# Norm weights folded into the merge, a lower lowest level, and the first score products of a chunk issued before the last one's means

## The reference, cut to what matters

```python
# gated linear attention (GLA: 4 heads of 64 keys; HGRN2: 4 heads of 128), chunk by chunk
b = cumsum(log_decay)
o_inter = (q * exp(b)) @ state
scores[i, j] = sum_d q[i, d] * k[j, d] * exp(b[i, d] - b[j, d])      # for j <= i
o = o_inter + scores @ v
state = state * exp(b_last) + (k * exp(b_last - b)).T @ v
y_gla = rms_norm(o, gla_norm_w) * silu(gr)                          # y_hgrn likewise
# Mamba-2: y = chunked scan of x, gated by silu(z)
y_ssm = rms_norm(y, ssm_norm_w)                                     # in 4 groups of 256 channels
merged = g0 * (y_gla @ w_br_gla) + g1 * (y_hgrn @ w_br_hgrn) + g2 * (y_ssm @ w_br_ssm)
```

## Time and profile before

| | us |
|---|---|
| median of 3 runs | 2038.89 |
| lowest, highest run | 2036.88, 2039.36 |
| span of the profiled execution | 2040.4 |
| what the page gives outside the span | nothing |
| TensorE busy | 1925.7 (94%) |
| VectorE busy | 1472.5 (72%) |
| ScalarE busy | 1048.0 (51%) |

### The profile page before, as it was taken

How to read it: one execution, slowest core, us unless ns; L and a number is a source line. 1 busy time by engine, 2 the same in 40 slices (tenths; PEclk the granted TensorE clock), 3 DMA queues, 4 the chain that set the end, 5 groups by cost and what they waited for, 6 DMA issues and landing times. The chain is left out here.

```text
span 2040.4 us, 26797 instructions
## 1 busy us (share of the span) xinstructions
PE 1925.7 (94%) x10602; PEld 1576.7 (77%) x10603; DVE 1472.5 (72%) x1687; ACT 1048.0 (51%) x1234; POOL 218.3 (11%) x173
## 2 busy tenths in 40 slices
PE   6999999999999999999998999995999999999993
PEld 5789888888977777777776888874788888888881
DVE  5876467667227888788775656556889988999875
ACT  5234344444224545444444334223777887888763
POOL 3310000000030000000001000012122222222210
PEclk9999999999999999999998999997999999999996
DMA  5242332432355557656537654543999999999986
GB/s 168 86 145 73 114 104 97 131 104 93 107 145 158 151 160 168 167 127 152 160 115 282 206 204 182 229 178 138 349 376 384 389 386 385 389 386 387 387 331 259
DMA packets 212415, 436.11 MB, mean 214 GB/s; under 512 B 28018, under 2 KB 151042, under 8 KB 184770
## 3 DMA queue, kind: packets, MB, share of 16 engines
q1 hardware_dynamic: 179394, 355.68, 50.3%
q10 hardware_dynamic: 20864, 53.49, 7.5%
q0 software_dynamic: 12032, 25.22, 3.2%
HBM read 369.67 MB, written 81.43 MB: 221 GB/s over the span
## 5 line engine op out<-in xcount | busy, mean ns | idle before, releaser
L1602 PE MATMUL psum<-h_hi,l_hi 128*128 128x512 f32 x384 | 158.5, 413 | 4.9 <-PEq L58 3.3
L1602 PE MATMUL psum<-h_lo,l_hi 128*128 128x512 f32 x384 | 159.8, 416 | 0.0
L1602 PE MATMUL psum<-h_hi,l_lo 128*128 128x512 f32 x384 | 157.9, 411 | 0.0
L2741 DVE TENSOR_TENSOR gu_lo<-up_raw,gu_hi 128x2048 fp32r<-128x2048 f32 x64 | 146.3, 2288 | 13.2 <-ACT gu_hi L2684 13.2
L2684 ACT CAST gu_hi<-up_raw 128x2048 fp32r<-128x2048 f32 x64 | 122.1, 1909 | 35.0 <-PE u_ps L2813 35.0
L1258 ACT COPY l_out<-psum 128x512 f32<-128x512 f32 x48 | 28.1, 585 | 170.3 <-PE psum L1602 162.3
L2457 PE MATMUL mpsum<-y_hi,wb_hi 128*128 128x512 f32 x256 | 103.3, 403 | 10.1 <-DVE y_lo L2217 9.1
L2813 PE MATMUL g_ps<-gu_hi,xeT_hi 128*128 128x512 f32 x256 | 105.0, 410 | 5.8 <-DVE xeT_lo L2750 5.8
L806 DVE TENSOR_TENSOR w_lo<-w_raw,w_hi 128x512 fp32r<-128x512 f32 x90 | 61.9, 689 | 65.5 <-ACT w_hi L662 65.5
L662 ACT CAST w_hi<-w_raw 128x512 fp32r<-128x512 f32 x90 | 55.7, 622 | 91.9 <-PE ps L931 91.4
L2457 PE MATMUL mpsum<-y_lo,wb_hi 128*128 128x512 f32 x256 | 101.7, 397 | 0.0
(11 more groups left out here) (465 smaller groups left out, 5419.0 us busy)
## 6 DMA issues: line engine op xcount, KB each, us to landing
up_raw<-moe SPq DMA_DIRECT2D x62, 1024.0 KB, 8.1
gate_raw_a<-moe SPq DMA_DIRECT2D x33, 1024.0 KB, 8.4
gate_raw<-moe SPq DMA_DIRECT2D x33, 1024.0 KB, 8.4
dn_raw_a<-moe SPq DMA_DIRECT2D x31, 1024.0 KB, 7.2
dn_raw<-moe SPq DMA_DIRECT2D x31, 1024.0 KB, 8.0
w_raw<-w_in SPq DMA_DIRECT2D x26, 1024.0 KB, 6.1
l_raw<-w_gates ACTq DMA_DIRECT2D x24, 512.0 KB, 5.4
s_gates<-l_out ACTq DMA_DIRECT2D x48, 256.0 KB, 4.0
```

What stands on the lines that cost most here:

```text
L1602: ins = nc.tensor.matmul(psum[:, bank, :], w[t % 2][:, k, :], x[:, k, half * 512:half * 512 + 512], start=i == 0, stop=i == LATE_MM - 1, s ...
L2741: nc.vector.tensor_tensor(gu_lo[p][:], gu_raw[p][:], gu_hi[p][:].bitcast(F32), ALU.subtract).then_inc(gu_ready, 1)
```

## The change

- **Norm weights.** `nw` and `nw_s` become one tile `y_w` that outlives the mixers. `gla_hgrn_out` and `ssm_out` no longer multiply with them: each is one operation over the chunk in place of 8. The merge multiplies instead: `upper_y` and `rest_y` apply them for each 128-channel row block, so each piece takes two operations of 512 columns in place of one of 1024, on ScalarE and on VectorE.
- **Lowest level.** At level h = 1 decay is taken relative to the later token. The query factor is then 1: `dec` makes half as many elements, ScalarE takes one exponential of half and copies the odd keys, VectorE has the key product only, and TensorE reads every second query straight from `q_in`.
- **Diagonal.** Since the copy at level 1 brings the odd keys undecayed, odd queries get their own token's score there; the mask of that level is widened. `diagonal` makes even queries alone: 12 products of the levels' form in place of 16 (in chunk 0, 6 in place of 8), into bank 1 alone, and `diagonal_in` is one copy in place of two. A further mask is made for it on GpSimd.
- **Order.** `relative(c+1, 0)`, `factors(c+1, 0)` and `(c+1, 1)`, two more `dec`, `diagonal(c+1)` and `level(c+1, 0)` move from the next body to the end of this one: on TensorE right behind `intra(c, 0)`, ahead of the filler and the means. On ScalarE `relative(c, 2)` moves ahead of `gla_hgrn_scale(c-1)`, and `relative(c+1, 0)` ahead of the copy of B. On VectorE `scores_in(0)` and `factors(2)` move ahead of `gla_hgrn_out`, and `scores_in(6)` ahead of the decayed queries. A level waits for one score copy less than before.

```diff
     NE = NL + 1
-    NS = NL + 2
+    NS = NL + 1
...
             def relative(c, lv):
                 i, h = NE * c + lv, LEVELS[lv]
+                if h == 1:
+                    act.wait_ge(qk_loaded[c % 2], 80 * turns(c))
+                    if c:
+                        act.wait_ge(sc_ready, NS * c)
+                    pairs = lambda ap: ap.rearrange("p (n w) -> p n w", w=2)
+                    nc.scalar.copy(pairs(k_one[:])[:, :, 1:2], pairs(flat(k_in[c % 2][:]))[:, :, 1:2])
+                    act.wait_ge(d_ready, i + 1)
+                    nc.scalar.activation(ex[i % 3][:, 0:CT * HALF], ex[i % 3][:, 0:CT * HALF], ACT.Exp).then_inc(e_ready, 1)
+                    return
...
             def body(c):
                 b, h0 = c % 2, PREFIX + PER_CHUNK * c
+                relative(c, 2)
                 if c:
                     gla_hgrn_scale(c - 1)
-                relative(c, 2)
...
                 nc.scalar.activation(wmat, wmat, ACT.Exp, scale=-1.0).then_inc(wexp_ready, 1)
+                if c < LAST:
+                    relative(c + 1, 0)
...
                 nc.scalar.activation(flat(ya), o_ps, ACT.Square).then_inc(sq_ready, 1)
                 if c < LAST:
-                    relative(c + 1, 0)
                     relative(c + 1, 1)
...
+                if lv == NL - 1:
+                    view = at[:].rearrange("p a (n w) -> p (a n) w", w=2)
+                    tt(out[:, 0:CT * HALF].unsqueeze(2), view[:, :, 1:2], view[:, :, 0:1], ALU.subtract).then_inc(d_ready, 1)
...
-                for h in range(NH):
-                    ins = stt(ya[:, h, :], g_in[:, h, :], nw[:, h:h + 1], ya[:, h, :], ALU.mult, ALU.mult)
-                ins.then_inc(ya_ready, 1)
+                tt(ya, g_in[:], ya, ALU.mult).then_inc(ya_ready, 1)
...
-                for k in range(8):
-                    ins = stt(yb[:, k, :], yt[:, k, :], nw_s[:, k:k + 1], rs2[:, k // 2, :], ALU.mult, ALU.mult)
-                ins.then_inc(yb_ready, 1)
+                by_group = lambda ap: ap.rearrange("p (g a) t -> p g a t", a=2)
+                tt(by_group(yb), by_group(yt[:]), rs2[:].unsqueeze(2).to_broadcast([P, SSM_GROUPS, 2, CH]), ALU.mult).then_inc(yb_ready, 1)
...
                 i0 = NE * c
-                factors(0)
-                factors(1)
                 if c:
                     dve.wait_ge(o_ready, c)
-                diagonal_in(0)
-                dec(i0 + 3)
-                diagonal_in(1)
-                dec(i0 + 4)
+                diagonal_in()
+                scores_in(0)
+                factors(c, 2)
                 if c:
                     gla_hgrn_out(c - 1)
-                else:
-                    late(3)
-                scores_in(0)
-                factors(2)
-                if c:
                     intra_in(c - 1, 1)
...
                 dec(i0 + 9)
                 dec(i0 + 10)
+                if c < LAST:
+                    factors(c + 1, 0)
+                    dec(i0 + 11)
                 late(h0 + 2)
...
                 intra_in(c, 0)
+                if c < LAST:
+                    factors(c + 1, 1)
+                    dec(i0 + 12)
...
             def body(c):
                 b = c % 2
-                diagonal(c)
                 if c:
                     intra(c - 1, 1)
-                fill(SLOT)
-                level(c, 0)
-                fill(SLOT)
+                fill(2 * SLOT)
                 level(c, 1)
...
                 intra(c, 0)
+                if c < LAST:
+                    diagonal(c + 1)
+                    level(c + 1, 0)
                 fill(SLOT)
...
-                nc.scalar.copy(y_hi[:, q * PK:(q + 1) * PK, :], y_part(p)).then_inc(y_hi_ready, 1)
+                for k in range(q * PK, (q + 1) * PK):
+                    ins = nc.scalar.activation(y_hi[:, k, :], y_part(p)[:, k - q * PK, :], ACT.Copy, scale=y_w[:, k:k + 1])
+                ins.then_inc(y_hi_ready, 1)
...
-                tt(y_lo[:, ks, :], y_part(p), y_hi[:, ks, :].bitcast(F32), ALU.subtract).then_inc(y_ready, 1)
+                for k in range(q * PK, (q + 1) * PK):
+                    ins = stt(y_lo[:, k, :], y_part(p)[:, k - q * PK, :], y_w[:, k:k + 1], y_hi[:, k, :].bitcast(F32),
+                              ALU.mult, ALU.subtract)
+                ins.then_inc(y_ready, 1)
```

More of the change, by code:

```diff
@@ L955, in late_bank, with mixers @@
     return 7
[L958 removed]
+def mixers(nc, io, dr, h_hi, h_lo, l_raw, l_hi, l_lo, w_place, xz_place, y_w, stored, early):
     LEVELS = [64 >> n for n in range(7)]
@@ L1215, in _ @@
             n = 0
-            for lv, h in enumerate(LEVELS):
+            for lv, (h, past) in enumerate([(h, h - 1) for h in LEVELS[:-1]] + [(1, 1), (1, 0)]):
                 nb = CH // (2 * h)
@@ L1227, in _ @@
                 pool.wait_ge(mask_sem, n)
-                nc.gpsimd.affine_select(out=view, in_=view, compare_op=ALU.is_ge, fill=0.0, base=h - 1,
+                nc.gpsimd.affine_select(out=view, in_=view, compare_op=ALU.is_ge, fill=0.0, base=past,
                                         pattern=[[2 * h, nb], [0, h]], channel_multiplier=-1).then_inc(mask_sem, 1)
@@ L1386, in _ @@
                 own.link(nc.vector.memset(k_lv[b][:], 0.0))
-            for lv in range(NL):
+            for lv, to in enumerate(mask + [mask_d]):
                 dve.wait_ge(mask_sem, 3 * lv + 3)
-                nc.vector.tensor_copy(mask[lv][:].rearrange("p (a h) -> p a h", h=HALF),
+                nc.vector.tensor_copy(to[:].rearrange("p (a h) -> p a h", h=HALF),
                                       mask_f[:].unsqueeze(1).to_broadcast([P, NH, HALF])).then_inc(mask_ready, 1)
-            dve.wait_ge(mask_ready, NL)
-            dve.wait_ge(ident_ready, 1)
-            own.link(nc.vector.tensor_copy(mask_d[:].rearrange("p (a h) -> p a h", h=CH),
-                                           ident[:].unsqueeze(1).to_broadcast([P, 4, CH])))
+            dve.wait_ge(mask_ready, NL + 1)
             dve.wait_ge(const_ready, 3)
@@ L1470, in factors, with body, diagonal_in @@
                     tt(ql[:, 2:8], q8[:, 2:8, :, h:2 * h], e6[:, :, :, h:2 * h], ALU.mult).then_inc(qk_ready, 1)
-                def diagonal_in(a):
-                    n = NS * c + a
+            def body(c):
+                b, h0 = c % 2, PREFIX + PER_CHUNK * c
+                def diagonal_in():
+                    n = NS * c
                     dve.wait_ge(sc_ready, n + 1)
@@ L1508, in body @@
                 dec(i0 + 5)
-                factors(3)
+                factors(c, 3)
                 if c:
@@ L1519, in body @@
                 dec(i0 + 6)
-                factors(4)
+                factors(c, 4)
                 late(h0)
@@ L1528, in body @@
                 dec(i0 + 7)
-                factors(5)
+                factors(c, 5)
                 late(h0 + 1)
                 scores_in(4)
-                factors(6)
+                factors(c, 6)
                 dve.wait_ge(xT_ready, c + 1)
@@ L1540, in body @@
                 tt(k_in[b][:], k_in[b][:], ex[(NE * c + NL) % 3][:].rearrange("p (a t) -> p a t", t=CH), ALU.mult).then_inc(qk_ready, 1)
+                scores_in(6)
                 dve.wait_ge(eb6_ready, c + 1)
@@ L1569, in _ @@
             late(1)
+            for lv in range(2):
+                factors(0, lv)
+                dec(lv + 3)
+            late(3)
             for c in range(NCH):
@@ L1607, in _, with one_of_two @@
             SLOT = LATE_MM // 3
+            def one_of_two(q, which):
+                return q[:].rearrange("p a (n w) -> p a n w", w=2)[:, :, :, which]
             def heads():
@@ L1636, in diagonal @@
                     pe.wait_ge(inter_used, c)
-                for half in range(2):
-                    for h, qa, a, _ in heads():
-                        if h // 4 == half:
-                            for r in (slice(0, HALF), slice(HALF, CH)) if c else (slice(0, CH),):
-                                ins = nc.tensor.matmul(sc_ps[half][r, (h % 4) * CH + r.start:(h % 4) * CH + r.stop],
-                                                       k_in[b][:, a, r], q_in[b][:, qa, r], start=True, stop=True, skip_group_check=True)
-                    ins.then_inc(sc_ready, 1)
+                ql = one_of_two(q_in[b], 0)
+                out = sc_ps[1].rearrange("p (a n) -> p a n", n=HALF)
+                for a in range(CT):
+                    n, q2 = (2 * a, ql[:, a:4:2, :]) if a < 2 else (a + 2, ql[:, a + 2:a + 3, :])
+                    for r in (slice(0, HALF), slice(HALF, CH)) if c else (slice(0, CH),):
+                        w = slice(r.start // 2, r.stop // 2)
+                        ins = nc.tensor.matmul(out[r, n:n + q2.shape[1], w], k_in[b][:, a, r], q2[:, :, w], start=True, stop=True,
+                                               skip_group_check=True)
+                ins.then_inc(sc_ready, 1)
             def ssm_state(c):
@@ L1765, in _ @@
             pe.wait_ge(const_ready, 3)
+            diagonal(0)
+            level(0, 0)
```

51 lines of the change are left out of this document (28 added, 23 removed).

## The result

The changed kernel takes 2048.31 us (median of 4 runs, 2046.09 to 2049.83), the kernel before 2038.1 beside it: a ratio of **1.0045** [1.0031, 1.006], slower by 0.45%. In a second set of 12 runs it was 2048.56, ratio 1.0043 [1.0027, 1.0058]. The forecast was 2041.0, in a range of 2033 to 2047. The profiled execution of the changed kernel took 2048.22 us, with a span of 2045.8 (2040.4 before). Two executions of the kernel before (2172 and 6764 us) and one of e17_best (2435 us) ran far longer than all others, and the ratios leave them out.

A forecast was written before the change was run, and what follows sets the result against it. TensorE, busy 94% of the span, was taken as the bound. Chunk terms of +2.0 us plus 0.15 for the merge gave +2.1 on the profiled 2040.4; against the median, 1.5 lower, 2041.0 us, range 2033 to 2047.

The forecast's parts named there:

- The chain up to `z_gated`: ScalarE's and VectorE's operations behind the means up to `z_gated`; claimed to end 1.89 us sooner.
- `intra` up by 0.93, `wmat` asked for that much sooner: The shorter diagonal ahead of `intra` lets the `wmat` load be issued 0.93 us sooner.
- lands 16.0 us later: The `wmat` load was taken to land 16.0 us after issue, so `wd` could start at 735.8.
- Even chunks were to cost +0.5: Per even chunk: 1.35 us shorter up to the turning of B, 1.87 longer behind it, net +0.5.
- Part B +1.87: From the turning of B to the next means, TensorE gains the next chunk's diagonal and level 0: +1.87 us.
- part A: From the means to the turning of B, where other engines' chain ends last; claimed 1.35 us shorter in chunk 2.
- The clock: Low clock behind stalls at `mean_b` or the turning of B: 1.4 to 1.6 us each, five of eight chunks.
- the slower rival: Clock lowered behind each of the 8 stalls at `mean_b` and the turning of B: 2045.8 us; chance 0.23.
- Chunk 0, +1.9: Chunk 0's body makes chunk 1's products, with no chain ahead of the turning of B to shorten: +1.9 us.
- The merge, 0.15: Two 512-column operations replace one of 1024 ahead of the first `y_lo`: +0.15 us; the other 15 pieces 0.
- the strided read of queries, 0: TensorE reading every second query at the lowest level: taken as 0, at most 3.2 us.

The follow-up runs named there:

- e17_best: Changed kernel with TensorE's diagonal and level 0 behind `intra` in their own chunk, both `l_raw` loads put off, `cbm` ahead of `wd`: 2010.58 us, 0.9876.
- e7_defer: Changed kernel with ScalarE's load into `l_raw` in even chunks put off until `wd` is computed: 2043.08 us, 1.0023.
- e15_before_cross: Kernel before, with the even chunks' load into `l_raw` issued behind the logarithm and exponential of `gla_hgrn_scale`: 2045.56 us, 1.0024.
- e14_pe_back: e7_defer with TensorE's diagonal and level 0 back in their own chunk's body, behind `intra`; other engines keep the new order: 2024.9 us, 0.993.
- a_again: The changed kernel itself, unaltered, measured once more beside the others: 2048.56 us, 1.0043.
- e5_split: Changed kernel with the `wmat` broadcast in two halves, the first asked for when the first part of `intra` is done: 2038.67 us, 1.0.
- e16_squares: Changed kernel with the old order, `cbm` ahead of `wd`, and the odd chunks' load into `l_raw` issued behind the squares: 2013.18 us, 0.987.
- e4_order_undone: Changed kernel with the old order; norm weights in the merge, lowest level and single diagonal stay: 2033.06 us, 0.9978.

## Why the prediction was wrong

By its own steps:

- **The chain up to `z_gated`** (`relative` ahead of Ln, one gate operation, `scores_in(0)` and `factors(2)` early): right. It said 1.89 us sooner; odd chunks show T+17.88 against T+19.78, and chunk 2 17.4 where 17.6 was forecast.
- **`intra` up by 0.93, `wmat` asked for that much sooner**: right, 4.82 behind the means instead of 5.74.
- **"lands 16.0 us later"**: this is the step that failed. The 16.0 was the median of a kernel in which, in even chunks, `l_raw` was asked for 0.98 us ahead and landed after 4.6 to 6.6 us. Moved up by 0.92, `wmat` goes out 0.04 us behind `l_raw`, and it landed 19.7 us later in chunk 2 and 18.4 in chunk 6 (16.5 in chunk 4). The prediction moved the issue and kept the landing, and never asked what else is issued at T+4.8. Even chunks were to cost +0.5; 2 and 6 cost +4.9 and +3.0. That is 6.9 us over the forecast for these two; the other chunks kept within 0.5 of theirs, and the eighth means came 7.6 us late (1070.08 against 1062.48) instead of 2.0. That the crossing costs time is shown in both directions (e7_defer, e15_before_cross). With it away the changed kernel is 4.7 us above the kernel before (1.0023), inside the range; it is what carried the time out of it. How late a single landing is also depends on scatter that stays unexplained.
- **Part B +1.87**: near in size, 32.5 and 31.9 us in chunks 3 and 5 instead of 31.0 and 30.3. (The prediction has chunk 3's turning of B at 801.02, which is the second of its weight loads. The first starts at 800.33, so part A is 27.3 us there and not 28.0; nothing in the sum rests on it.) The prediction set it against part A's gain, since "the diagonal products are now made long before". e14_pe_back shows that part A's gain didn't need it: the products can stay in the body, behind `intra`, and `z_gated` is as early. So the move is a pure price: 19.0 us in all, with what the stalls behind it do to the clock. The sum netted two things of which one was not the cause of the other.
- **The clock**: the slower rival had the place (L1680 and L1721) and the direction, but counted stretches. Their number stayed at 5, but chunk 2's became 9.9 us instead of 3.4, with a stall of 7.9 us at its begin, and chunk 6's became 6.5.
- **Chunk 0, +1.9**: the first means came 1.6 us later. But those of a_again came at 661.74, 3.5 us later still, so one profile can't tell this term.
- **The merge, 0.15, and the strided read of queries, 0**: nothing speaks against either. On ScalarE a piece takes 1.23 us from start to start instead of 0.95 (1099.75 to 1102.21 for two of them, 1092.23 to 1094.13 before), within the 0.2 to 0.3 more that the prediction named. A level at h = 1 took 0.84 us from start to start as another does (758.36 to 759.20 in chunk 2, and 755.47 to 756.29 for level 5). The wait for the first `y_lo`, 9.07 in the earlier trace rows, is now 9.18, so 0.11 of it reaches TensorE:

```profile
1102.73 0.76 PE L2486 MATMUL mpsum<-y_hi,wb_hi 128*128 128x512 f32 x1 [9.18 <-DVE y_lo L2244]
```

The account by ratios, times 2038: norm weights -1.6, lowest level -2.9, new order on VectorE and ScalarE (with the load put off, and the two groups of matmuls behind `intra`) -9.8, the two groups of matmuls in front of the means +19.0, the crossing +4.5; together +9.2. By the intervals each is uncertain by 3 to 5 us, so that of the first two only the sum (-4.5) is clear of zero, and the last three were measured one upon the other, not each alone.

**Left open**: why `wmat` takes 16.5 to 19.3 us in chunk 5 of every kernel here with a single broadcast, the old one too, with no `l_raw` beside it, why its landings scatter by 3 us in even chunks without a crossing, and what half a broadcast would take alone: in e5_split the second half always ran beside the first.

## What to carry to other kernels

A transfer's time from issue to landing holds only for what was in flight beside it: when a change moves an issue, by even a microsecond, list every other issue within the transfer's time, on all queues, and see who now goes first. Work that can run while an engine waits is free there and has its full price elsewhere; move it only if something shown to be late waits for its result, and price the move by itself, not netted against a gain that other parts of the change bring. And look first at what stands behind a late transfer by program order alone: `cbm` did not need `wmat`, and putting it ahead was worth 17 us in the old order.

## What the hardware showed that was not expected

- Two loads asked for within 0.04 us: 1 MB in 512-byte rows and 0.5 MB. The smaller one took 14.3 to 19.5 us, though with a lead of 0.98 us it takes 4.6 to 6.6, and the larger one up to 19.7 instead of 16.0. For 8 us of that the smaller one's queue moved 0.13 MB beside the other's 0.60. In e7_defer, with no load on it, the same queue moved nothing from 728 to 736 us while the broadcast ran, and a store of 256 KB asked for then took 10.6 us.
- Splitting the broadcast and asking for one half 8.3 us earlier doesn't bring the halves in quickly: in the even chunks the first took 17.3 to 18.9 us and the second 14.7 to 17.7 (e5_split), where all of it takes 16.2 to 16.8 (e7_defer).
- Where TensorE no longer waited for another engine ahead of `mean_b` or the turning of B, the granted clock stayed at 1.00 (2.4 GHz) through all seven chunks (e16_squares, e17_best); around and behind the 7.9 us stall of chunk 2 it was at 0.50 (1.2 GHz) for 9.9 us. The length of a stall alone doesn't tell: with 4.62 us in front of the turning of B in chunk 4 of e4_order_undone the clock stayed at 1.00, and with 2.85 us in front of `mean_b` in chunk 3 of the kernel before it fell.
